# Attention stage: the half-swap copies split between two DMA-issuing engines, with a wait before the next weights

## The reference

```python
def rotary(t, positions):
    half = t.shape[-1] // 2
    ...
    t1 = t[..., :half].astype(jnp.float32)
    t2 = t[..., half:].astype(jnp.float32)
    return jnp.concatenate([t1 * cos - t2 * sin, t2 * cos + t1 * sin], axis=-1)
...
    proj = (h @ w_in).reshape(B, S, N_DIL_GROUPS, 3, A_HEADS, A_HEAD_DIM)
    for gi, (window, dil) in enumerate(DILATED_GROUPS):
        q = (rotary(proj[:, :, gi, 0], positions) * scale).transpose(0, 2, 1, 3)
        k = rotary(proj[:, :, gi, 1], positions).transpose(0, 2, 1, 3)
        v = proj[:, :, gi, 2].astype(jnp.float32).transpose(0, 2, 1, 3)
```

## Time and profile before

| | us |
|---|---|
| median of 3 runs | 2624.65 (2623.46 to 2626.0) |
| the profiled execution | 2624.83 |
| span of its instructions | 2623.1 |
| TensorE busy | 2456.6 (94% of the span) |
| VectorE busy | 1209.0 (46%) |
| ScalarE busy | 588.0 (22%) |
| GpSimd busy | 490.8 (19%) |
| TensorE idle in the attention stage, put down to another engine | 9.2 |

### The profile page before, as it was taken

One profiled execution on the slowest core, in us unless ns is written; L12 is line 12 of the kernel. 1 busy time (PEld: TensorE's weight loads), 2 busy tenths in 40 slices (PEclk: granted clock), 3 DMA queues, 4 the chain that ended last, 5 costly groups with the idle time before them and its releaser, 6 DMA issues. The chain is left out here.

```text
span 2623.1 us, 38415 instructions
## 1 busy us (share of the span) xinstructions
PE 2456.6 (94%) x14213; PEld 1443.2 (55%) x14214; DVE 1209.0 (46%) x2562; ACT 588.0 (22%) x1357; POOL 490.8 (19%) x488
## 2 busy tenths in 40 slices
PE   5999999998999999999998999999899999999996
PEld 3878787776854333333334658576764433333332
DVE  3846566574444333332245544635443443333326
ACT  1131131413111111111113443334211111111111
POOL 2504224240001111111100212222001111111110
PEclk9999999999999999999998999999999999999998
DMA  7726354363468999999964131221629999999967
GB/s 255 208 72 193 113 153 121 106 184 119 194 231 331 388 421 418 410 420 398 418 252 169 52 91 53 68 72 40 232 102 340 364 418 420 402 420 414 396 272 292
DMA packets 173625, 657.36 MB, mean 251 GB/s; under 512 B 25300, under 2 KB 87100, under 8 KB 118296
## 3 DMA queue, kind: packets, MB, share of 16 engines
q1 hardware_dynamic: 117936, 409.57, 40.8%
q10 hardware_dynamic: 20280, 136.27, 12.9%
q0 software_dynamic: 35248, 109.36, 12.0%
HBM read 616.27 MB, written 53.52 MB: 255 GB/s over the span
## 5 line engine op out<-in xcount | busy, mean ns | idle before, releaser
L1724 DVE TENSOR_SCALAR core_oT<-moe_tx,moe_by,moe_plus 128x128 f32<-128x128 f32 x360 | 123.0, 404 | 543.8 <-PE moe_tx L1989 543.7
L2028 PE MATMUL moe_py<-weights_w,moe_hT 128*32 128x512 f32 (+2 forms) x1296 | 312.7, 596 | 0.9 <-ACT moe_hT L1444 0.9
L2014 PE MATMUL moe_ph<-weights_w,core_oT 128*32 128x512 f32 (+2 forms) x1216 | 303.6, 615 | 2.5 <-issue 2.5
L2014 PE MATMUL moe_pr<-weights_w,core_oT 128*64 128x512 f32 (+2 forms) x864 | 274.2, 601 | 10.5 <-DMA core_ring<-in_expert_w_dram 6.3
L1523 POOL DMA_INDIRECT y_rows<-moe_ysb,moe_yidx x90 | 102.2, 1136 | 929.7 <-DVE moe_idx L1716 563.1
L1444 ACT COPY moe_hT<-moe_th 128x256 f32<-128x256 f32 x90 | 33.6, 373 | 917.1 <-PE moe_th L1977 917.1
L2657 PE MATMUL gdn_pj<-core_hT,core_ring 128*128 128x512 f32 x512 | 226.3, 596 | 5.2 <-ACTq L2391 5.2
L2657 PEld LDWEIGHTS gdn_pj<-core_hT,core_ring 128*128 128x128 f32 x512 | 96.8, 191 | 122.1 <-issue 122.1
L2014 PEld LDWEIGHTS moe_pr<-weights_w,core_oT 128*64 128x64 f32 (+2 forms) x864 | 92.0, 141 | 125.5 <-issue 124.9
L2028 PEld LDWEIGHTS moe_py<-weights_w,moe_hT 128*32 128x32 f32 (+2 forms) x1296 | 92.4, 128 | 120.6 <-issue 113.3
L2028 PE MATMUL moe_py<-core_ring,moe_hT 128*32 128x512 f32 (+2 forms) x416 | 145.3, 596 | 2.6 <-DVE moe_ysb L1861 2.6
(11 more groups left out here) (455 smaller groups left out, 4173.4 us busy)
## 6 DMA issues: line engine op xcount, KB each, us to landing
weights_w<-in_expert_w_dram SPq DMA_DIRECT2D x160, 1024.0 KB, 14.9
weights_w<-in_expert_w_dram ACTq DMA_DIRECT2D x92, 1024.0 KB, 10.5
core_ring<-in_expert_w_dram SPq DMA_DIRECT2D x54, 1024.0 KB, 14.7
core_hT<-in_expert_w_dram SPq DMA_DIRECT2D x48, 1024.0 KB, 13.9
core_ring<-in_attn_w_in_dram SPq DMA_DIRECT2D x36, 1024.0 KB, 6.3
weights_w<-y_rows SPq DMA_DIRECT2D x32, 1024.0 KB, 13.3
core_ring<-in_expert_w_dram ACTq DMA_DIRECT2D x30, 1024.0 KB, 10.1
attn_ada_w<-in_ada_w_dram POOLq DMA_DIRECT2D x64, 384.0 KB, 4.2
```

The source lines that it names most:

```text
L1724: last = nc.vector.tensor_scalar(xT[:, b, k], tx[1][:, k - 4], by[:, k:k + 1], plus[:, k:k + 1], ALU.mult, ALU.add)
L2014: last = nc.tensor.matmul(ph[p % 2][at, :], xT[:, p % 2, k, at], w13[ew.up_place(n)[0]][:, :, k], start=k == 0, stop=k == KT - 1)
L2028: last = nc.tensor.matmul(py[n][at, :], hT2[:, p % 2, k, at], w2[ew.down_place(m)[0]][:, k, half(n)], start=k == 0, stop=k == 1)
```

## The change

Of the four swap pieces SyncE issues the first two (destination partitions 0 to 63), and ScalarE the other two. ScalarE gets its own waits for `raw` and does this right behind its last copy of the sub-step, ahead of everything else in its program. SyncE then waits until all four pieces have landed before it goes on to the next load of weights.

```diff
@@ SyncE, swapped(i, s)
                 sp.wait_ge(chain_kept, nth(i, s, 4, 4) + 8)
                 sp.sem_inc(turn_seen, 1)
-                for d in range(4):
-                    e = d ^ 1
-                    sp.dma_start(swp[32 * d:32 * d + 32], raw[32 * e:32 * e + 32]).then_inc(swp_in, 16)
+                for d in range(2):
+                    sp.dma_start(swp[32 * d:32 * d + 32], raw[32 * (d ^ 1):32 * (d ^ 1) + 32]).then_inc(swp_in, 16)
+                sp.wait_ge(swp_in, 64 * NSUB * i + 64 * (s + 1))
+                sp.sem_inc(turn_seen, 1)
@@ ScalarE, new
+            def swapped(i, s):
+                act.wait_ge(pair_joined, nth(i, s, 2, 2) + 2)
+                act.wait_ge(first_joined, nth(i, s, 1, 1) + 1)
+                act.wait_ge(chain_kept, nth(i, s, 4, 4) + 8)
+                for d in range(2, 4):
+                    act.dma_start(swp[32 * d:32 * d + 32], raw[32 * (d ^ 1):32 * (d ^ 1) + 32]).then_inc(swp_in, 16)
@@ ScalarE, quad(i, following)
                         if u:
                             keep_u3(i, u)
                             lay_21(i, u)
+                        swapped(i, u)
                         continue
```

## The result

The changed kernel takes 2635.27 us (median of 5 runs, 2629.06 to 2637.8) against 2625.28 us for the kernel before, run beside it (median of 5, 2623.46 to 2627.74). The ratio is 1.0031, with a 95% interval of 1.0017 to 1.0045: slower by 4.5 to 11.8 us. The profiled execution took 2635.27 us with a span of 2633.6 us, 10.5 us more than before.

A forecast was written before the change was run, and what follows sets the result against it. TensorE, 94% busy, was taken as the bound, only its attention-stage waits winnable (at most 9.7 us). 0 (turns 0 to 2) - 2.4 (turn 3) + 0 (ScalarE) = -2.4 us gave 2622.3 us, range 2618 to 2628.5.

The forecast's parts named there:

- rival (c): Attention, u = 1: chunk 4 moved onto adaLN loads makes load 7 late; 3.6 to 6.0 us slower; chance 0.14.
- Part 2: Weights wait for the pieces: head gain and load 7's loss give 0 for turns 0 to 2.
- from a landing above about 5 us on: Load 7's landing time after issue beyond which the slower outcome was said to decide.
- within 0.4: GpSimd's sums of u = 2 start where they did in turn 1, within 0.4 us.
- Part 1: Swap at u = 0: two pieces issued from ScalarE save 1.0 us at VectorE, bounds 0.5 and 1.25.
- Part 3: Turn 3, u = 0: weights held back behind the late last piece win 2.4 us, other end 0.
- Part 4: ScalarE's queue: its issues ahead of `keep_m1` cost 0; other bound 0.4 us at each of eight places.
- The chunk 8 slack: Sub-step 4's weights, read by v products: 3.0 us of slack against 1 to 1.5 us of delay.
- a stop costs a little more than the wait shown: TensorE's stops at product 6, sub-steps 3 and 4: 0.16 us added to each of eight waits.

The follow-up runs named there:

- experiment 3, u = 0: Kernel before with SyncE's wait for the four pieces in sub-step 0 alone: 2627.46 us against 2629.28 us, ratio 0.9996.
- experiment 5: Kernel before plus seven dependent ScalarE copies at the attention stage's end, so later stages start later: 2633.35 us against 2627.77 us, ratio 1.0023.
- both `BEHIND` kernels: Kernel before and changed kernel, each with two adaLN adds moved from u = 1 to u = 2: 1.0005 (2628.48 us) and 1.0027 (2635.32 us) against before.

## Why the prediction was wrong

The prediction said 2622.3 us and gave rival (c), which came true, a chance of 0.14.

**Part 2 failed, in its "0 for turns 0 to 2".** The place was named rightly. Holding back chunk 3 and chunk 4 makes the head of the chain of adaLN loads late, and the sum has nothing for it. In turns 0 to 2 the stops grew by 0.7, 1.7 and 1.4 us, 3.8 in all, where 0 stood; rival (c) had 1.5 us a turn. The wait alone costs the whole loss (1.0036), and with 256 KB in place of the megabyte it costs nothing (0.9989), so the cause is shown.

What was mis-sized is this. Load 7 was taken to land after 4.4 us; it landed after 4.6, 5.3 and 3.8 us in turns 0 to 2 (3.4 in turn 3), a mean of 4.6, so that term was nearly right. Left out were load 8 right behind it (5.5 us in turn 1 of the changed kernel, up to 8.6 us with the wait at u = 1 alone), the later issue of load 7 (by 1.1, 2.1 and 1.4 us from the start of the v product, through chunk 3), and load 10, which fell behind chunk 5. In turn 2 load 7 landed about as fast as before, and its late issue did the damage. So (c)'s own mechanism, a late landing of load 7, is that of turns 0 and 1, and its switch ("from a landing above about 5 us on") was met in turn 1 alone.

 The argument against (c), that chunk 4's tail lay beside load 7 before, took a tail for the whole: chunk 4 went out 4.2 to 5.0 us ahead of load 7 before and 1.7, 2.6 and 2.7 us ahead in turns 0 to 2 of the changed kernel. The waits after the first piece were mis-sized too: chunk 3 went out 4.2 to 5.7 us behind the first piece of u = 0 (2.8 before, 3.1 in turn 3), not about 3.6, and chunk 4 5.1 to 6.4 us behind that of u = 1. The sums of u = 2 did start late (1.4 us in turn 1, against "within 0.4"), but that part alone costs nothing (experiment 3, u = 0).

**Part 1 failed in its size.** Its 1.0 us at VectorE supposed that the four issues set the landing. At u = 4 the last adaLN load is over and chunk 8 goes out only behind the pieces. There SyncE's four pieces have landed 4.2 us after the first issue; in the kernel with the split only it is 3.9 to 4.0 us in turns 0 to 2 (5.0 in turn 3), with the last issue only 0.8 us behind the first in place of 1.8. The saving is 0.3 us at most, below the lower bound of 0.5; the rest goes into longer landings (2.8 to 3.2 us for SyncE's two, 2.3 to 2.4 before). The Trainium skill (DMA: Bandwidth & Descriptors, Issuing engines are not separate DMA queues), which the prediction weighed, limits the gain to the issue time; the trace agrees and is far below that limit. At u = 0 VectorE's wait for the swap was 1.76, 2.19, 0.94 and 1.12 us in turns 0 to 3 (1.63, 1.61, 1.62 and 4.00 before), so in turns 0 and 1 the gain was negative; about 0.6 was forecast for all.

**Part 3 was right in size at the head, too large at the stops, and wrong in its cause.** In turn 3 VectorE's wait fell from 4.00 to 1.12 us (2.9 us, where 2.4 stood) and load 16 came 2.1 us earlier, but TensorE's stops fell only from 4.4 to 3.1 us, by 1.3 (to 2.1 us with the split only). The holding back of the weights has no part in it: with the wait at u = 0 alone the last piece of turn 3 still landed 4.5 us after its issue and load 16 came at 29.5 us. The late piece at u = 5 of turn 1 landed after 4.5 us in the changed kernel too, with nothing behind it. It is the split that helps (the kernel with the split only shows it), but not by making the issues fast: SyncE's second issue at u = 0 of turn 3 took 1.35 us and ScalarE's 1.21 in the changed kernel. With four pieces from SyncE, one issue there takes 0.89 to 1.66 us in all eleven such kernels, and the pieces behind it wait, so that the last goes out 2.2 to 3.0 us behind the first (1.8 to 2.0 us at most other places). With the split no piece stands behind the slow issue, and all four are out within 0.8 us.

What the slow issue lies beside can be read from the traces. In each of the fourteen profiles a packet of 16 KB of another DMA queue runs at this place, of the kind that the profile calls `instruction`. The DMA queues of the kernel before between 507.5 and 508.5 us have it (packets, MB, share of the DMA engines):

```profile
q8 instruction: 1, 0.02, 6.0%
```

It took from 507.51 to 508.46 us, and the slow issue from 507.76 to 508.83. The packet's place against the pieces moves from kernel to kernel, by 0.9 us, and the end of the slow issue moves with it: it comes 0.37 us behind the packet's end in ten of the eleven kernels and 0.93 us behind it in the other, and with the split one of the issues ends 0.37 us behind it too. Such a packet also lies among the pieces of u = 5 of turn 1, where the last one has landed 5.0 to 6.3 us after the first issue in every kernel, and not 4.2. No run moved or removed the packet, so this link is read and not shown by an experiment. Why the last piece of u = 0 of turn 3 then needs 4.1 to 5.2 us from its own issue to its landing in nine of the eleven (2.6 in the other two) stays open.

**Part 4 held.** ScalarE's issues took 0.61 us in the median, and `keep_m1` ran at 212.55, ahead of `product_6` at 213.76. One wait of 0.6 us, at 580.1 us (sub-step 5 of turn 3), is the price.

**The chunk 8 slack and the clock.** No wait for the v chunks appeared. The clock stood in no term: "a stop costs a little more than the wait shown" misses that a stop of about 2 us can bring a stretch of half clock with it. In the changed kernel that is 1.7 us of the 4.3. The stop of the same length at 550.6 us of the kernel before brought none, so its rows gave no price for it.

**What stays open.** The mechanism accounts for 4.2 us in the profiled execution: 3.8 us of stops in turns 0 to 2, less 1.3 us in turn 3, and 1.7 us of dip. The runs give 4.5 to 11.8 us. The 6 us of the later stages are not the work of the change (experiment 5), but which share of the measured 10 us is chance of the executions isn't shown. The kernel before had medians from 2625.28 to 2629.28 us beside the other kernels, and single executions on one chip from 2623.76 to 2631.25 us; the one beside the changed kernel is the lowest of these medians. Also open is how much the late issue of load 7 and how much the late landings add, as no run holds back chunk 3 and chunk 4 by different amounts.

## What to carry to other kernels

A wait that holds back a big transfer doesn't remove its traffic but moves it: list what small, latency-bound loads it will then lie beside, and price each of them at the worst landing that the trace shows, above all if they head a chain. Then go one step further: a load that is late may lose its place ahead of another big transfer, as load 10 did here. So write down which big transfer each small load precedes, and by how many us; the margins of 1.0 us here were gone with delays of 1.5 to 3.6 us. A second issuing engine saves only as much as issuing set the landing: compare the last landing with the last issue where nothing else moves. When one instruction is slow at one place of every execution, look for a packet of an unexpected queue beside it. And slack made at one sub-step of such a chain moved the stop to the next one three times here (both `BEHIND` kernels, chunk 5 later), so count stops over all sub-steps before a change is called a gain.

## What the runs showed of the hardware

- Four 128 KB copies within SBUF take 4.2 us from one issuer and 3.9 to 4.0 us from two, with no load beside them (u = 4, turns 0 to 2), though the issues shrink from 1.83 to 0.77 us.
- A megabyte issued 0.6 us ahead of them in the same queue makes their landings 6.4 to 9.5 us, and one issue of SyncE was 2.24 us long. The megabyte then needs 9.7 to 11.1 us itself.
- A megabyte issued together with a 384 KB load of another queue needed 9.8 us itself, and the second 384 KB load beside it 8.6 us (4.1 us beside 256 KB).
- Stops of TensorE of about 2 us were followed by 3.4 us at 1.2 GHz in some cases (256.1 us in the changed kernel, 106.6 and 560.6 us with the wait only, 404.0 us with the wait at u = 1), and not in others of the same length (the one at 550.6 us before).
- One DMA issue in each kernel that fell beside a 16 KB packet of kind `instruction` took 0.89 to 1.66 us in place of 0.6, and ended 0.37 us behind the packet's end in ten of the eleven kernels in which SyncE issues all pieces.
